# Other slots for scores and turns in two of four attention passes, and the pair's bank emptied in the slot of its last product

## What is computed

```python
def token_mixer(h, w_in, conv_w, q_gain, k_gain, sink, w_o):
    proj = h @ w_in
    cb, cc, cu, q, k, v, ga, gb = jnp.split(proj, ...)
    y_a = cb * dwconv3(cc * cu, conv_w)
    q = rms_norm(q.reshape(b, s, N_Q_HEADS, HEAD_DIM), q_gain)
    k = rms_norm(k.reshape(b, s, N_KV_HEADS, HEAD_DIM), k_gain)
    y_b = windowed_gqa(q, k, v, sink)     # 128 queries against a band of 384 keys
    merged = jax.nn.sigmoid(ga) * y_a + jax.nn.sigmoid(gb) * y_b
    return merged @ w_o
```

## Time and profile before

| | before |
|---|---|
| median of 3 runs | 795.26 us (792.97 to 796.44) |
| profiled execution, time | 794.5 us |
| profiled execution, span from the first to the last instruction | 792.7 us |
| mean granted clock of TensorE | 0.995 |
| TensorE busy | 779.8 us (98%) |
| its weight loads | 650.5 us (82%) |
| VectorE busy | 522.6 us (66%) |
| ScalarE busy | 373.7 us (47%) |
| GpSimd busy | 378.8 us (48%) |

### The profile page before, as it was taken

The page is one execution under the profiler, slowest core; times in us unless marked ns, Lnnn a source line. Parts: engine busy times, 40 slices in busy tenths (PEclk is TensorE's granted clock), DMA queues, the critical chain, the costliest instruction groups (busy, mean ns, idle before and its releaser), DMA issues.

```text
span 792.7 us, 10498 instructions
## 1 busy us (share of the span) xinstructions
PE 779.8 (98%) x3761; PEld 650.5 (82%) x3761; DVE 522.6 (66%) x717; ACT 373.7 (47%) x662; POOL 378.8 (48%) x232
## 2 busy tenths in 40 slices
PE   7999999999999999999999999999999999999997
PEld 6888887888888888888889988888888888888886
DVE  4757996687667766798548699888888888000000
ACT  7564667545655475555445544433344433222220
POOL 3775344534443544437771355445544455444440
PEclk9999999999999999999999999999999999999999
DMA  8935162435243434236331133332233332223311
GB/s 310 384 132 187 39 226 67 150 107 193 73 160 107 162 104 155 84 108 186 106 107 54 55 106 106 106 105 70 89 106 106 106 106 66 81 93 120 132 57 37
DMA packets 83279, 96.03 MB, mean 121 GB/s; under 512 B 2674, under 2 KB 77610, under 8 KB 83242
## 3 DMA queue, kind: packets, MB, share of 16 engines
q1 hardware_dynamic: 79018, 93.44, 35.2%
q10 hardware_dynamic: 4224, 2.10, 0.9%
HBM read 93.43 MB, written 2.10 MB: 121 GB/s over the span
## 4 chain that ended last, share of the span: by engine, by line
PE 88%; DVE 6%; ACT 2%; SPq 1%; issue 1%; DMA 1%; DVEq 0%; ACTq 0%
PE bank L868 26%; PE bank L870 26%; PE bank L869 26%; PE bank L1034 2%; PE bank L1062 2%; PE bank L1045 2%; DVE pt_lo L1415 1%; DVE a_buf L1439 1%; PE bank L952 1%; PE bank L953 1%; DVE sm L1401 1%; PE bank L957 1%; DVE prob L1394 1%; SPq L405 1%; DMA w_raw<-in_ffn_conv_b_dram 1%
## 5 line engine op out<-in xcount | busy, mean ns | idle before, releaser
L868 PE MATMUL bank<-h_hi,w_hi 128*128 128x512 f32 (+1 forms) x760 | 293.6, 386 | 0.0
L869 PE MATMUL bank<-h_lo,w_hi 128*128 128x512 f32 (+1 forms) x760 | 291.3, 383 | 0.0
L870 PE MATMUL bank<-h_hi,w_lo 128*128 128x512 f32 (+1 forms) x760 | 291.2, 383 | 0.0
L470 POOL TENSOR_TENSOR w_lo<-w_raw,w_hi 128x1024 fp32r<-128x1024 f32 x74 | 190.8, 2599 | 186.5 <-ACT w_hi L579 186.5
L477 POOL TENSOR_TENSOR w_lo<-w_raw,w_hi 128x512 fp32r<-128x512 f32 x92 | 128.4, 1419 | 174.5 <-ACT w_hi L579 170.2
L579 ACT ACTIVATE w_hi<-w_raw 128x1024 fp32r<-128x1024 f32 x120 | 122.5, 1052 | 97.4 <-PE bank L870 97.3
L870 PEld LDWEIGHTS bank<-h_hi,w_lo 128*128 128x128 f32 x760 | 142.8, 188 | 28.7
L868 PEld LDWEIGHTS bank<-h_hi,w_hi 128*128 128x128 f32 x760 | 142.9, 188 | 26.9
L869 PEld LDWEIGHTS bank<-h_lo,w_hi 128*128 128x128 f32 x760 | 142.9, 188 | 26.4
L868 PE MATMUL bank<-g_hi,w_hi 128*128 128x512 f32 x176 | 69.2, 393 | 0.0
L870 PE MATMUL bank<-g_hi,w_lo 128*128 128x512 f32 x176 | 68.6, 390 | 0.0
(11 more groups left out here) (202 smaller groups left out, 1085.0 us busy)
## 6 DMA issues: line engine op xcount, KB each, us to landing
w_raw<-in_w_in_dram SPq DMA_DIRECT2D x23, 1024.0 KB, 5.2
w_raw<-in_w_up_dram SPq DMA_DIRECT2D x21, 1024.0 KB, 4.9
ada<-in_w_ada_dram SPq DMA_DIRECT2D x32, 512.0 KB, 5.0
ada<-in_w_ada_dram SPq DMA_DIRECT2D x32, 256.0 KB, 6.2
w_raw<-in_w_down_dram SPq DMA_DIRECT2D x8, 1024.0 KB, 4.7
w_raw<-in_w_o_dram SPq DMA_DIRECT2D x4, 1024.0 KB, 6.5
w_raw<-in_w_down_dram SPq DMA_DIRECT2D x4, 768.0 KB, 4.1
x_nat<-in_x_dram SPq DMA_DIRECT2D x4, 512.0 KB, 5.0
```

Of the source, the lines that this page charges most:

```text
L470: pool.tensor_tensor(lo_of(n, u), raw(n)[:, :, u * P:(u + 1) * P], hi_of(n, u), SUB).then_inc(lo_ready, 1)
L868: pe.matmul(dst, w_h, rhs_hi, start=first, stop=False)
L869: pe.matmul(dst, w_h, rhs_lo, start=False, stop=False)
L870: return pe.matmul(dst, w_l, rhs_hi, start=False, stop=last)
```

## The change

Passes two and three (`g` of 1 and 2) get other slots. Scores were at 0, 5, 10, 15 and are now at 0, 4, 8, 12; turns were at 6, 11, 16, 21 and are now at 6, 10, 14, 18. Their eight `gemv` steps were in every even slot from 4 to 18 and are now at 7, 10, 13, 15, 17, 19, 20 and 22. `LATE` was 1 in passes two to four and is now 0 in all, so in pass four it is the only thing that changes.

```diff
-        SCORE = [(5, 9, 13, 16), (0, 5, 10, 15), (0, 5, 10, 15), (0, 4, 8, 12)]
-        TURN = [(11, 15, 18, 21), (6, 11, 16, 21), (6, 11, 16, 21), (6, 10, 14, 17)]
+        SCORE = [(5, 9, 13, 16), (0, 4, 8, 12), (0, 4, 8, 12), (0, 4, 8, 12)]
+        TURN = [(11, 15, 18, 21), (6, 10, 14, 18), (6, 10, 14, 18), (6, 10, 14, 17)]
...
-        LATE = [0, 1, 1, 1]
-        EVEN = {2 * n + 4: n for n in range(KT)}
-        GEMV_AT = [{6: 0, 11: 1, 12: 2, 13: 3, 15: 4, 16: 5, 19: 6, 21: 7}, EVEN, EVEN,
+        LATE = [0, 0, 0, 0]
+        SPACED = {7: 0, 10: 1, 13: 2, 15: 3, 17: 4, 19: 5, 20: 6, 22: 7}
+        GEMV_AT = [{6: 0, 11: 1, 12: 2, 13: 3, 15: 4, 16: 5, 19: 6, 21: 7}, SPACED, SPACED,
                    {7: 0, 10: 1, 11: 2, 13: 3, 15: 4, 16: 5, 18: 6, 19: 7}]
```

## The result

Both kernels were run 22 times side by side. The changed kernel took 796.44 us (794.07 to 798.76), the kernel before 794.57 us (792.15 to 796.44). The ratio is 1.0021, with a 95% interval from 1.0012 to 1.0029: the change costs some 1.7 us. That is small, but it is not nothing, and the forecast was that it would be nothing. The time lies in the range of the prediction; the sign of the change was missed.

A forecast was written before the change was run, and what follows sets the result against it. TensorE, busy 98% of the span, was taken as the bound. The terms -0.58 + 0.54 + 0 + 0 = -0.04 us on 794.5 us turned the median of 795.26 into 795.2 us, range 793.2 to 798.0.

The forecast's parts named there:

- The waits that go: Passes two and three, slot 18: TensorE's longer steps before `values` vanish, -0.58 us in all.
- The waits that come: Passes two and three: VectorE falls behind between slots 6 and 10, one step of 0.27 us each, +0.54 us.
- The ceiling: Passes two and three: a better order of the same work can give back only 0.58 us, 0.07% of 794.5.
- Scores and turns in slots of their own: Passes two and three: turns no longer share slots with scores, same matmuls issued; costed at nothing.
- `LATE` to 0: Slots 7, 12, 16, 19: ScalarE and VectorE wait for `pv_done` ahead of the slot's remaining work; nothing on the path, 0.
- Pass four: From slot 18: merge starts 0.5 to 2.2 us later, cover 2.1 us; 0, bound +0.3 or +1 us.
- Rival 4: Tail of pass four: `LATE` costs 0.3 to 1 us ahead of the output projection, 795.5 to 796.2 us; chance 0.05.
- The loads: SyncE's weight loads wait for later `gemv` steps but land in time, margins 1.5 us or more; 0, bound +1 us.
- The query's turn: Slot 19: ScalarE has two high halves ahead of the query's drain, margin 0.3 us; 0, bound +0.5 us a pass.
- The collision: Passes two and three, slots 6 to 10: VectorE's two-input instructions blocked by GpSimd's subtractions, about 1.05 us each.

The follow-up runs named there:

- run 22: Not a run's label, only a count: changed kernel and kernel before were each run 22 times side by side; 796.44 and 794.57 us, ratio 1.0021.
- the fastest version: Changed kernel with `LATE` 1 in pass four and step 0 of the sums in slot 4, not 7, in passes two to four; 793.96 us, ratio 0.9985.
- the run with its part alone: Kernel before with ScalarE's part of the emptying (`heads_low`) in the slot of the last product in pass four, VectorE's part as before; ratio 1.0011.

## Why the prediction was right or wrong

**The waits that go** held. Both steps in slot 18 are gone, -0.58 us.

**The waits that come** held in place and order of size: predicted near 179 and 261 us at 0.27, found at 179.6 and 261.5 at 0.41, and 0.11 at the step behind, which I had left out of the sum. Passes two and three are 0.05 us longer each, against -0.02 forecast. That this is so near is in part luck, by the next point. The pattern taken from pass four of the kernel before was not quite the one that came: there step 0 of the sums took 1.66 us (331.96) and L1437 0.49; in pass two of the changed kernel step 0 took 0.79 (169.57), and L1437, now beside a subtraction, 1.51. I did not try which of the two makes 0.41 of 0.27.

**The ceiling** of 0.58 us, "the first thing that I hold to", was too low, and *Scores and turns in slots of their own*, put at nothing, was a gain. In slot 16 of the kernel before, four score matmuls stood behind the turn's transposes; in slot 13 of the changed one they stand alone. Kernel before and changed:

```profile
196.26 0.85 PE L1034 MATMUL bank<-k_st,q_st 128*128 128x256 f32 x4
196.96 0.39 PE L868 MATMUL bank<-h_hi,w_hi 128*128 128x512 f32 x1
```

```profile
188.21 0.64 PE L1034 MATMUL bank<-k_st,q_st 128*128 128x256 f32 x4
188.69 0.40 PE L868 MATMUL bank<-h_hi,w_hi 128*128 128x512 f32 x1
```

They took 0.70 us (0.71 in pass three) and now take 0.48. Some 0.09 of it comes back, as now a projection matmul stands behind the transposes and its step is 0.31. No step of the 0.22 is over 0.23 us by itself, so a count of the longer steps misses it. With 0.05 behind the old wait of slot 18, pass two is -0.32 - 0.05 - 0.13 + 0.41 + 0.11 = +0.02, measured 0.06, and pass three -0.26 - 0.06 - 0.14 + 0.52 = +0.06, measured 0.05. In the fastest version the two passes give back 0.96 us (162.63 for 163.59), more than the ceiling.

**Pass four is where it failed.** The step "*`LATE` to 0*" said of ScalarE and VectorE that "TensorE asks for neither within the slot", and put the price at 0. The queue behind `heads_low` in slot 16 holds ScalarE's last high half, for GpSimd, whose chain has no idle time from there to the projection's tiles. I had looked for who waits for the two engines one step on, not two. The step "*Pass four*" priced VectorE's merge, 0.5 to 2.2 us later; it was 1.5 us later (375.95 for 373.88, less 0.56) and covered, as said. GpSimd's low halves were named in half a sentence, "+1 if GpSimd's low halves slip too", with no row; they slipped, and it cost 1.26 us. Rival 4 had this case at 0.3 to 1 us, less than it cost, and a chance of 0.05. The cover that decided, 0.74 us for tile 3, could be read beforehand from two rows of the trace of before (377.23 and 379.58).

**The loads** came later, in the order that the step on them said, by 2.5 us or so more: at 200.75 us (198 forecast) and in the group from 214.97 on (212.5). I had written that ScalarE's rows would name no DMA. They do, once in each pass, 0.81 us at 221.72 and 1.87 in pass three:

```profile
304.62 1.06 ACT L579 ACTIVATE w_hi<-w_raw 128x1024 fp32r<-128x1024 f32 x1 [1.87 <-DMA w_raw<-in_w_in_dram]
```

Nobody was late for it. **The query's turn**: no step at slot 19; the square ended at 208.49 and TensorE turned it at 208.68, a margin of 0.2 us where I had 0.3.

**The collision** was weighed as a matter of passes two and three. The page "SBUF — State Buffer" of the Trainium skill, section "Who interferes with whom", cited there, says that the order of issue decides who blocks, so its rule holds in both directions, and I had used one: there a late VectorE stalls, here GpSimd does. The chain's instructions of 0.62 us took up to 1.60 beside VectorE's steps.

## What to carry to other kernels

A queue entry that is moved ahead of others delays all of them: follow each to its consumer's consumer, until an engine with idle time is met, and read the cover there from two rows. A chain that never idles hands on every delay at its front, and the time for which another engine's instructions block it counts as part of it. A stall that one edit removes may be worth nothing until the backlog that the edit creates elsewhere is taken away too.

## What the runs showed of the hardware

VectorE's two-input steps out of SBUF and GpSimd's subtractions did not run side by side here: one waited out the other, and the wait stands in the record of the one that waits. So the price of a delay is not its size. 0.7 us more on ScalarE cost 0 (GpSimd would have been blocked until 365.5 anyway), and so did 0.94 more in the run with its part alone; a product of 128x8 took 1.25 us (365.29 to 366.54), until GpSimd's subtraction ended at 366.51; and step 5 inside the chain made it 1.5 us longer in either of two places, for which TensorE waited 1.15 us more. VectorE's L1415, which reads a bank and one tile of SBUF, was not held up: its two took 1.28 us beside a subtraction (368.75, changed kernel) and 1.29 while GpSimd stood idle (326.56, kernel before). Between 142 and 306 us VectorE's busy time rose from 118.86 to 125.90 us in the changed kernel for the same work in the same time, and GpSimd's fell from 73.93 to 68.23, so their busy shares are in part waiting.

The scatter of a few us between executions is not spread over them. In the twelve profiles the first mark of pass two lies between 139.9 and 143.7 us, though the code ahead of it is the same in all; kernels with the same tables repeat their passes to within some 0.1 us. That is why stretches of one profile told more here than medians of twelve runs.
